# Three units of seven products in the gates' pairs of a float32 block kernel, and the branch sum on VectorE

## What is computed

```python
proj = xn @ w_in[l]
xa, xpool, xsc, qkv, f_logit, gate_logits = jnp.split(proj, split_pts, axis=-1)
...
branches = jnp.einsum('bskw,kwd->bskd', ys, w_branch[l])
gates = jax.nn.sigmoid(gate_logits.reshape(b, s, N_BRANCH, d))
merged = jnp.sum(gates * branches, axis=2)
x = x + merged @ w_out[l]
```

## Time and profile before

| | us |
|---|---|
| median of 3 runs | 2455.98 (2455.34 to 2456.57) |
| the profiled execution | 2456.58 |
| its span, first to last instruction | 2454.8 |
| mean granted clock of PE in it | 0.999 |

### The profile page before, as it was taken

The page is one execution under the profiler, slowest core; times in us unless marked ns, Lnnn a source line. Parts: engine busy times, 40 slices in busy tenths (PEclk is TensorE's granted clock), DMA queues, the critical chain, the costliest instruction groups (busy, mean ns, idle before and its releaser), DMA issues.

```text
span 2454.8 us, 28949 instructions
## 1 busy us (share of the span) xinstructions
PE 2442.9 (100%) x11683; PEld 2042.7 (83%) x11683; DVE 1791.8 (73%) x1704; ACT 1236.9 (50%) x1314; POOL 117.0 (5%) x95
## 2 busy tenths in 40 slices
PE   9999999999999999999999999999999999999999
PEld 8888878888888888888888888788888888888887
DVE  5775577777755785776775558886788878887887
ACT  5545544444444544544444448875554444444543
POOL 0410010110110000000000010000200000000000
PEclk9999999999999999999999999999999999999999
DMA  8555455666655565665665656444565665665654
GB/s 256 174 183 180 163 187 191 203 192 198 238 183 187 188 206 189 198 197 183 203 198 189 206 172 191 152 152 160 179 196 193 201 197 183 206 202 191 203 189 154
DMA packets 233907, 467.18 MB, mean 190 GB/s; under 512 B 14192, under 2 KB 25984, under 8 KB 233390
## 3 DMA queue, kind: packets, MB, share of 16 engines
q1 hardware_dynamic: 232222, 460.09, 57.7%
q10 hardware_dynamic: 1552, 5.25, 0.6%
HBM read 463.20 MB, written 2.10 MB: 190 GB/s over the span
## 4 chain that ended last, share of the span: by engine, by line
PE 96%; DVE 2%; ACT 1%; issue 1%; POOL 0%; DMA 0%; ACTq 0%; DVEq 0%; POOLq 0%
PE acc L1741 13%; PE acc L1737 13%; PE acc L1738 13%; PE acc L459 10%; PE acc L450 10%; PE acc L452 10%; PE acc L479 5%; PE acc L485 2%; PE tp L479 2%; PE sd L479 2%; PE acc L1795 2%; PE acc L1792 2%; PE acc L1791 2%; PE sd L485 1%; PE tp L485 1%; PE sd L1795 1%
## 5 line engine op out<-in xcount | busy, mean ns | idle before, releaser
L435 DVE TENSOR_TENSOR wlo<-raw,whi 128x2048 fp32r<-128x2048 f32 (+1 forms) x384 | 884.8, 2305 | 538.9 <-ACT whi L427 537.9
L427 ACT ACTIVATE whi<-raw 128x2048 fp32r<-128x2048 f32 (+1 forms) x384 | 724.9, 1889 | 795.5 <-PE acc L1741 339.2
L1737 PE MATMUL acc<-whi,opA_hi 128*128 128x512 f32 x840 | 327.7, 390 | 0.0
L1738 PE MATMUL acc<-whi,opA_lo 128*128 128x512 f32 x840 | 327.6, 390 | 0.0
L450 PE MATMUL acc<-whi,opA_hi 128*128 128x512 f32 x768 | 304.6, 397 | 0.0
L452 PE MATMUL acc<-whi,opA_lo 128*128 128x512 f32 x768 | 299.4, 390 | 0.0
L1741 PE MATMUL acc<-wlo,opA_hi 128*128 128x512 f32 x840 | 226.0, 390 | 1.9 <-DVE wlo L435 1.9
L1737 PE MATMUL acc<-whi,opB 128*128 128x512 f32 x536 | 209.5, 391 | 0.0
L1738 PE MATMUL acc<-whi,opB 128*128 128x512 f32 x536 | 208.6, 389 | 0.0
L459 PE MATMUL acc<-wlo,opA_hi 128*128 128x512 f32 x768 | 192.6, 392 | 0.2 <-DVE wlo L435 0.2
L1741 PEld LDWEIGHTS acc<-wlo,opA_hi 128*128 128x128 f32 x840 | 158.1, 188 | 36.0 <-DVE wlo L435 3.2
(11 more groups left out here) (421 smaller groups left out, 3661.2 us busy)
## 6 DMA issues: line engine op xcount, KB each, us to landing
raw<-in_w_in SPq DMA_DIRECT2D x66, 1024.0 KB, 5.3
raw<-in_w_mlp_up SPq DMA_DIRECT2D x64, 1024.0 KB, 5.3
raw<-in_w_mlp_down SPq DMA_DIRECT2D x64, 1024.0 KB, 5.0
raw<-in_w_in SPq DMA_DIRECT2D x120, 512.0 KB, 4.7
raw<-in_w_gate SPq DMA_DIRECT2D x88, 512.0 KB, 3.8
raw<-in_w_up SPq DMA_DIRECT2D x88, 512.0 KB, 4.7
raw<-in_w_down SPq DMA_DIRECT2D x88, 512.0 KB, 4.6
raw<-in_w_out SPq DMA_DIRECT2D x32, 1024.0 KB, 5.0
```

The lines of the kernel that those rows point to most:

```text
L427: eng.activation(whi[:, j % SPL, k, 0:cols], raw[:, j, k, 0:cols], ACT.Copy).then_inc(hi_split, share(k))
L435: eng.tensor_tensor(wlo[:, j % SPL, k, 0:cols], raw[:, j, k, 0:cols], whi[:, j % SPL, k, 0:cols].bitcast(F32), ALU.subtract).then_inc(lo_s ...
L1737: pe.matmul(acc[:, b, m, :], hi[:, 2 * v + a, rows], whi[:, s, 2 * a + b, :], start=first and a == 0, stop=False)
L1738: pe.matmul(acc[:, b, m, :], lo[:, 2 * v + a, rows], whi[:, s, 2 * a + b, :], start=False, stop=False)
```

## The change

In pairs 1 to 5 unit 1 too is a unit of seven; pair 0 keeps units 3 and 5. The third set of operand sums is made in pair 0: its sums by VectorE behind the low split of unit 0 and ahead of the last branch product of chunk 0, its high part by ACT and its low part by VectorE behind unit 1. It takes the place in memory where `yz` stood, and the gates' `yz` moves to where `t_sum` lies.

In the gates' pairs with three units of seven, VectorE makes the own low parts ahead of the sums of the weights; in pair 0 and in all other stages the sums stay ahead. ACT tells PE of the high parts of the first two sums by themselves (`t_high`), and PE waits for these at index 3 and for the rest at index 5; this holds in all stages.

The sum of the branches is made by VectorE, each add right behind its `branch_part`; POOL's `merge` is gone.

The diff without its renamings (`yz` to `p.yz`, `a_hi[op][:, x]` to `a_part`), the new semaphore's name, and `SUMS0`, which becomes 3:

```diff
--- before.py
+++ after.py
@@ -109,7 +109,8 @@
 PAIR_UNITS = KT // 2
 GATE_SEVEN, DOWN_SEVEN = (3, 5), (3, 5)
 FIRST_SEVEN, QUARTERS = (3, 5), 3
-BRANCH_SEVEN, LATER = (3, 5), 3
+BRANCH_SEVEN, LATER = (1, 3, 5), 3
+BRANCH_PLACES = (3, 5, 1)
 
 
 def readers_before(run, who):
@@ -269,7 +270,9 @@
         a_hi = [at("ag_hi", 148, [P, 2, 4, P], F32R), at("ad_hi", c1, [P, 2, 4, P], F32R)]
         a_lo = [at("ag_lo", 152, [P, 2, 4, P], F32R), at("ad_lo", c1 + 4, [P, 2, 4, P], F32R)]
         vw = at("vw", 168, [P, 2, NW])
-        yz = at("yz", c1 + 36, [P, 2, NW])
+        yzs = [at("yz", 148, [P, 2, NW]), at("yz2", c1 + 36, [P, 2, NW])]
+
+        a_third = [at("a_third_hi", c1 + 36, [P, 4, P], F32R), at("a_third_lo", c1 + 38, [P, 4, P], F32R)]
         q_sums = [at("q_sum", 166, [P, NW]), at("q_sum2", 148, [P, NW]), at("q_sum3", c0 + 1.5, [P, NW])]
         rstd_neg = at("rstd_neg", 150, [P, MT])
         stat2 = lambda k: smalls2[:, k * 48:(k + 1) * 48].rearrange("p (s c) -> p s c", s=3)
...
@@ -540,8 +543,8 @@
                 self.op, self.places, self.chunk, self.turned = op, places, chunk_, turned_
 
 
-        PAIRS0 = [Pair(n, "sigmoid", (G_LOOP + 5 * (n // 2) + 2 * (n % 2)) * UN, PAIR_UNITS, BRANCH_SEVEN, 1,
-                       BRANCH_SEVEN, (n // 2, n % 2), 0) for n in range(2 * LATER)]
+        PAIRS0 = [Pair(n, "sigmoid", (G_LOOP + 5 * (n // 2) + 2 * (n % 2)) * UN, PAIR_UNITS, 
+                       BRANCH_SEVEN if n else BRANCH_SEVEN[1:], 1, BRANCH_PLACES, (n // 2, n % 2), 0) for n in range(2 * LATER)]
         PAIRS1 = [Pair(n, "scaled", (G_DLOOP + 8 * (n // 2)) * UN + n % 2 * PAIR_UNITS, PAIR_UNITS, FIRST_SEVEN, 1,
                        FIRST_SEVEN, (n // 2, n % 2), 0) for n in range(2 * QUARTERS)]
         PAIRS = []
@@ -569,6 +572,11 @@
             p.seven_units = [q.unit + v for q in ahead for v in q.seven]
             p.q_sum = q_sums[0 if p.kind == "sigmoid" else 1 if p.kind == "scaled" else 2]
             p.t_sum = t_sums[p.kind != "sigmoid"]
+            p.yz = yzs[p.kind != "sigmoid"]
+
+        def a_part(low, op, x):
+
+            return a_third[low][:, :, :] if x == 2 else (a_hi, a_lo)[low][op][:, x]
 
         def last_seven(p, v):
 
...
@@ -909,19 +917,6 @@
             pool.wait_ge(head_sum, 1)
             head_squares(1)
 
-            def merge(n):
-
-                for k in range(1, NB):
-                    run = R_GATE0 + n * 2 * NB + NB + k
-                    pool.wait_ge(read_dve, readers_before(run + 1, "D") * MT)
-                    if k > 1:
-                        pool.wait_ge(merged_ready, n * (NB - 1) + k - 1)
-                    pool.tensor_tensor(xres[:, :, chunk(n)], xres[:, :, chunk(n)], stage[:, :, :],
-                                       ALU.add).then_inc(merged_ready, 1)
-
-            for n in range(UN):
-                merge(n)
-
             def gained(run, n, gain=gainB):
 
                 pool.wait_ge(read_dve, readers_before(run + 1, "D") * MT)
@@ -1007,13 +1002,13 @@
                 act.activation(seven_hi[:, 0, :], raw[:, u % RAW, 0, :], ACT.Copy)
                 act.activation(seven_hi[:, 1:3, :], raw[:, u % RAW, 2:4, :], ACT.Copy).then_inc(hi_split, 1)
                 act.wait_ge(t_made, 3 * n + 1)
-                act.activation(seven_hi[:, 3:5, :], p.t_sum[:, 0:2, :], ACT.Copy)
+                act.activation(seven_hi[:, 3:5, :], p.t_sum[:, 0:2, :], ACT.Copy).then_inc(t_high, 1)
                 act.wait_ge(t_made, 3 * n + 3)
                 act.activation(seven_hi[:, 5:7, :], p.t_sum[:, 2:4, :], ACT.Copy).then_inc(hi_split, 1)
 
             def sums_high(op, x, n):
                 act.wait_ge(a_made, n + 1)
-                act.activation(a_hi[op][:, x, :, :], a_sums[n >= SUMS0][:, :, :], ACT.Copy).then_inc(a_high, 1)
+                act.activation(a_part(0, op, x), a_sums[n >= SUMS0][:, :, :], ACT.Copy).then_inc(a_high, 1)
 
             def first_sums_high(i, j):
 
@@ -1253,6 +1248,8 @@
                             hi_unit(act, (p.unit + v) // UN, v % UN)
                         if p.chunk[1] and v == 0:
                             sigmoids(PAIRS0[p.n - 1])
+                        if p.n == 0 and v == 1:
+                            sums_high(1, 2, 2)
                         if v == p.units - 1:
                             q_copy(p)
                 for j in range(UN):
...
@@ -1786,8 +1783,13 @@
                         pe.wait_ge(op_lo, T_HID2 + p.turned * MT)
                 pe.wait_ge(a_low, sums_made(p, v))
                 for done, products in ((1, own), (2, made)):
-                    pe.wait_ge(hi_split, u * HV + done)
+                    if done == 1:
+                        pe.wait_ge(hi_split, u * HV + 1)
                     for bank, (a_h, a_l), i, alone in products:
+                        if i == 3:
+                            pe.wait_ge(t_high, sevens_before(p, v) + 1)
+                        if i == 5:
+                            pe.wait_ge(hi_split, u * HV + 2)
                         pe.matmul(bank, a_h, seven_hi[:, i, :], start=alone and first, stop=False)
                         pe.matmul(bank, a_l, seven_hi[:, i, :], start=False, stop=False)
                     pe.wait_ge(lo_split, u * HV + done)
@@ -2225,6 +2227,11 @@
                 for m in range(MT):
                     dve.tensor_tensor(stage[:, m, :] if k else xres[:, m, chunk(n)], acc[:, run % 2, m, :],
                                       gates[:, k, m, :], ALU.mult).then_inc(read_dve, 1)
+                if k:
+
+                    dve.wait_ge(read_dve, readers_before(R_GATE0 + n * 2 * NB + NB + k + 1, "D") * MT)
+                    dve.tensor_tensor(xres[:, :, chunk(n)], xres[:, :, chunk(n)], stage[:, :, :],
+                                      ALU.add).then_inc(merged_ready, 1)
 
 
             def seven_low(p, v):
@@ -2235,19 +2242,26 @@
                 if last_seven(p, v):
                     dve.wait_ge(lo_split, last_seven(p, v) * HV)
                 dve.wait_ge(a_low, sums_made(p, v))
-
-                dve.tensor_tensor(p.t_sum[:, 0:2, :], w[:, 0:4:3, :], w[:, 1:2, :].to_broadcast([P, 2, NW]),
-                                  ALU.add).then_inc(t_made, 1)
-                dve.wait_ge(t_made, 3 * n + 1)
-                dve.tensor_tensor(p.t_sum[:, 2, :], p.t_sum[:, 0, :], w[:, 3, :], ALU.add).then_inc(t_made, 1)
-                dve.wait_ge(t_made, 3 * n + 2)
-                dve.tensor_tensor(p.t_sum[:, 3, :], p.t_sum[:, 2, :], w[:, 2, :], ALU.add).then_inc(t_made, 1)
-                if last_seven(p, v):
-                    dve.wait_ge(units_used, last_seven(p, v))
-                dve.wait_ge(hi_split, u * HV + 1)
-                dve.tensor_tensor(seven_lo[:, 0, :], w[:, 0, :], seven_hi[:, 0, :].bitcast(F32), ALU.subtract)
-                dve.tensor_tensor(seven_lo[:, 1:3, :], w[:, 2:4, :], seven_hi[:, 1:3, :].bitcast(F32),
-                                  ALU.subtract).then_inc(lo_split, 1)
+                def weights_sums():
+
+                    dve.tensor_tensor(p.t_sum[:, 0:2, :], w[:, 0:4:3, :], w[:, 1:2, :].to_broadcast([P, 2, NW]),
+                                      ALU.add).then_inc(t_made, 1)
+                    dve.wait_ge(t_made, 3 * n + 1)
+                    dve.tensor_tensor(p.t_sum[:, 2, :], p.t_sum[:, 0, :], w[:, 3, :], ALU.add).then_inc(t_made, 1)
+                    dve.wait_ge(t_made, 3 * n + 2)
+                    dve.tensor_tensor(p.t_sum[:, 3, :], p.t_sum[:, 2, :], w[:, 2, :], ALU.add).then_inc(t_made, 1)
+
+                def own_low():
+                    if last_seven(p, v):
+                        dve.wait_ge(units_used, last_seven(p, v))
+                    dve.wait_ge(hi_split, u * HV + 1)
+                    dve.tensor_tensor(seven_lo[:, 0, :], w[:, 0, :], seven_hi[:, 0, :].bitcast(F32), ALU.subtract)
+                    dve.tensor_tensor(seven_lo[:, 1:3, :], w[:, 2:4, :], seven_hi[:, 1:3, :].bitcast(F32),
+                                      ALU.subtract).then_inc(lo_split, 1)
+
+
+                for part in (own_low, weights_sums) if len(p.seven) > 2 else (weights_sums, own_low):
+                    part()
                 dve.wait_ge(hi_split, u * HV + 2)
                 dve.wait_ge(t_made, 3 * n + 3)
                 dve.tensor_tensor(seven_lo[:, 3:7, :], p.t_sum[:, :, :], seven_hi[:, 3:7, :].bitcast(F32),
...
@@ -2388,7 +2402,7 @@
                 if j % 2:
                     operand_low(1, j // 2, j // 2)
                 else:
-                    operand_sums(1, BRANCH_SEVEN[j // 2], j // 2, 0)
+                    operand_sums(1, BRANCH_PLACES[j // 2], j // 2, 0)
             def merged_lo(c):
                 turned_lo(dve, T_MERGED + c * MT, opA_hi, opA_lo, c * CT)
 
@@ -2403,6 +2417,10 @@
                             lo_unit(dve, (p.unit + v) // UN, v % UN)
                         if p.chunk[1] and v == 0:
                             sum_gates(PAIRS0[p.n - 1], [(0, 1), (1, 0), (1, 1)])
+                        if p.n == 0 and v == 0:
```

(21 more changed lines are left out.)

## The result

| | us |
|---|---|
| changed kernel, median of 5 runs | 2466.70 (2466.11 to 2468.47) |
| kernel before, median of 5 runs | 2455.88 (2455.19 to 2456.57) |
| ratio, 95% interval | 1.0045 (1.0034 to 1.0056) |
| the profiled execution of the changed kernel | 2466.89, span 2465.2 |

A forecast was written before the change was run, and what follows sets the result against it. PE's number of products plus the few places where PE stands bound the kernel; 17.6 us of stalls, less 3.4 of products, less 5.0 of present losses, gave +9.2 on the 2455.98 median: 2465.2, range 2458 to 2471.

The forecast's parts named there:

- third unit, 15 matmuls fewer: Pairs 1 to 5: unit 1 goes from 24 matmuls to 21, saving PE 3.4 us.
- ten waits at units 3 and 5: Pairs 1 to 5: PE waits 0.56 us plus 0.12 restart for the last low parts, ten times: 6.8 us lost.
- unit 1 of pairs 1, 3, 5: ACT's late read of the previous pair's last bank delays the low parts; wait 1.88, restart 0.24, three times: 6.4 us.
- unit 1 of pairs 2, 4: The last branch product and its add delay the sums; wait 1.27 plus restart 0.12, twice: 2.8 us.
- unit 0 of pair 0: Low split slightly late, third operand's sums delay the last branch product: 1.6 us lost in place of 3.79.
- losses of before that go: Delays from POOL's add holding VectorE's low split: 3.79 at pair 0, 0.68 at pairs 2 and 4, 0.5 at transposes; 5.0 us removed.
- E + 9.86: Units 3 and 5: last low parts ready 9.86 us after the preceding plain unit's start E, wanted at E + 9.30.
- Rival A: Clock falls to half behind some of the six longer waits, 1.66 us each; three give 2470.2; chance 0.18.
- B: The ten short waits at units 3 and 5 vanish through shorter hand-overs: 2458.4, counted as the same; chance 0.10.
- C: Last low parts are ready in time in every unit of seven, leaving 1.6 of stalls: 2449.2; chance 0.07.
- D: VectorE's branch add takes 2.4 us in place of 1.22, making nine units late by 0.5 each: 2469.7; chance 0.03.
- With the sums first this would be some 0.2: Unit 1 of pairs 2 and 4: weight sums ahead would cost some 0.2, because the own low parts would be late.

The follow-up runs named there:

- experiment with two units of seven: Kernel before, two units of seven and POOL's adds kept, only the own low parts put ahead of the sums in the gates' pairs: 2460.26 us.
- the sums first and the other two moves: Changed kernel with weight sums before own low parts, third operand's sums behind chunk 0's last branch product, and two adds per chunk 0 to 2 later: 2448.60 us.
- the kernel with one wait for the high parts: Changed kernel without t_high, so PE waits once for the high parts of all four sums: 2467.09 us.
- the kernel with the order at units 3 and 5 alone: Changed kernel with own low parts first only at units 3 and 5, weight sums first at unit 1: 2458.47 us.

## Why the prediction was right

The time, 2466.7 for 2465.2, and the mechanism hold. Point by point, each cost being the unit's stretch less 4.76 or 5.44:

| step | forecast | measured |
|---|---|---|
| third unit, 15 matmuls fewer | -3.4 | -3.4 (4.76 for 5.44) |
| ten waits at units 3 and 5 | 6.8 | 7.2 (nine of 0.66 to 0.70, one of 1.04) |
| unit 1 of pairs 1, 3, 5 | 6.4 | 6.0 |
| unit 1 of pairs 2, 4 | 2.8 | 2.8 |
| unit 0 of pair 0 | 1.6 | 1.6 |
| losses of before that go | -5.0 | -3.35 |
| sum | +9.2 | +10.8 |

The last term is 2.17 for unit 0 of pair 0 and 0.68 for pairs 2 and 4, both measured, and 0.5 for the transposes, of which 0.38 is recorded. The sum, 17.6 - 3.4 - 3.35 = 10.8, is the measured difference. That the stalls alone come out at 17.6 as forecast is partly luck: two terms were off by 0.4, one up and one down. The 7.2 holds the single unit of 1.04, and the 6.4 booked a restart of 0.12 behind both parts of the wait. Measured is one: in pair 1 the last low matmuls start at 379.84, 1.86 after 374.12 + 3.86, and the unit loses 1.98. The restart behind the first part is covered, since VectorE sets the end of the second.

*The chain.* Worked out link by link from rows of another order, it gave E + 9.86; the last low parts began at E + 7.52 = 388.38 and ended at 390.67, E + 9.81. The experiment with two units of seven shows that the order alone is enough to make it, and the one with the sums first that it goes with the order. What had been taken from a single place, the restart of 0.12, held too.

*The one term that was off* is the loss of before. The prediction put "Stall and restart are 2.13, the clock the other 1.66" and removed both. The 1.66 were in the one profile it had, not in the two taken later, and a mean clock of 0.999 is on record for a quarter of the executions, so the median does not have them; the gain of the branch sum alone is 2.6 where 4.7 would include them. Without them the term is 3.35, and the forecast would have been 2466.9. The profiled execution stood 0.6 above the median at a mean clock of 0.999, which could have been the hint.

*The clock.* Rival A did not come: no fall in the changed kernel's profile and a mean of 1.000 in its five executions, with three units that lose 2.0 each. The longest single wait in them is 1.13. "The trace disagrees, so falls are a rival" has to be put more narrowly: a stall of 1.86 us was followed by half clock in one profile of five. By the Trainium skill, "TensorE: Matmul & The Clock Gate", section "Why this matters for your kernels", that one should not be either. No run here shows what decides.

*Rivals B, C and D.* B is out, the short waits did not vanish. C did not come either, since the last low parts are late in all fifteen units; a time near its 2449.2 takes the sums first and the other two moves (2448.60). D is out, since VectorE's add takes 1.22 as priced:

```profile
L2233 DVE TENSOR_TENSOR xres<-xres,stage 128x1024 f32<-128x1024 f32 x12 | 14.7, 1225 | 0.4
```

*"With the sums first this would be some 0.2"*: the stretch is 5.22, 0.46 over, of which 0.17 is recorded as a wait.

*Open.* Unit 5 of pair 2 lost 1.04 in place of 0.68 in the profiled execution. The excess lies in one link, the first hand-over from ACT to VectorE: the own low parts start 0.48 after the end of ACT's second copy, where the other nine units have 0.13. The same unit in the kernel with one wait for the high parts has the same 0.48 and loses 1.03, and unit 5 of pair 0 in the kernel with two units of seven (1.06) has it too. In the kernel with the order at units 3 and 5 alone no unit has it. Why is not settled.

## What to carry to other kernels

Where several engines hand a small buffer set round, count the path from the moment the buffer is free to the last part that is wanted, not the load: work that needs nothing of the buffer (here the sums of the weights) belongs ahead of the wait for it. A step that an idle engine does for a busy one can hold the busy one up for longer than the busy one needs for it: an add of 2.4 us on POOL kept VectorE's low split for 2.20 more (4.49 for 2.29), and the same add on VectorE takes 1.22. The move alone gained 2.6 us; VectorE had gaps for the adds, and putting two of three later took away the last waits. And a loss that stands in one profiled execution is to be looked for in a second one before it is booked as removable.

## What the runs showed of the hardware

A wait costs PE more than the idle time that its row shows: 0.68 us for recorded 0.40, 0.46 for 0.17, 2.17 for 1.86, so 0.28 to 0.31 more. Instruction durations on VectorE and ACT do not change with the order (1.22, 0.69, 2.28 and 1.06, where no add of POOL runs beside them), so that a chain of fourteen links, added up from rows of the kernel before, came out within 0.05 us for unit 3 of pair 1. One of its links, ACT to VectorE, was 0.48 in place of 0.13 in one of the ten units 3 and 5 of the changed kernel. An add of POOL beside VectorE stretched a low split from 2.29 to 4.49 and a sum of the weights from 0.69 to 2.78. A fall of the granted clock from the upper to the lower level (2.4 to 1.2 GHz) followed a stall of 1.86 us in one of five profiled executions, and lasted 3.4 us; a mean clock of 0.999 was seen in 24 of 89 executions of the kernels with that stall and in none of 68 without it.
